# The wide depthwise convolution of a hybrid layer, moved from VectorE to TensorE as products over shifted copies

## The reference, cut to what matters

```python
proj = x @ w_in                      # GLU | q,k,v | output gate | beta | decay | branch gates
u  = glu[:, :512] * sigmoid(glu[:, 512:])
cv = causal_dwconv(conv_hist, u, w_dw) + b_dw      # 512 channels, 31 taps, per group of tokens
A  = silu(layer_norm(cv)) @ w_conv_out             # branch A
q, k, v = split(silu(causal_dwconv(qkv_hist, qkv, w_short)))       # 4 taps
q, k = l2_norm(q) * 128 ** -0.5, l2_norm(k)
o, s_new = gated_delta_rule(q, k, v, beta, logdecay, s0)           # 4 heads of 128 x 128
B  = (rms_norm(o) * silu(og)) @ w_dn_out           # branch B
h  = layer_norm(alpha * x + (sigmoid(ga) * A + sigmoid(gb) * B) @ w_o)
# then cross-attention over 256 memory tokens, and a squared-ReLU MLP of width 4096
```

## Time and profile before

| | us |
|---|---|
| median of 3 runs (1341.56 to 1355.39) | 1348.65 |
| profiled execution, its own time | 1354.72 |
| its span, first to last instruction | 1352.9 |
| PE busy in the span | 1216.4 (90%) |
| DVE busy | 728.7 (54%) |
| ACT busy | 410.0 (30%) |
| POOL busy | 418.0 (31%) |
| mean granted TensorE clock | 0.937 of full |

### The profile page before, as it was taken

How to read it: one execution, slowest core, us unless ns; L and a number is a source line. 1 busy time by engine, 2 the same in 40 slices (tenths; PEclk the granted TensorE clock), 3 DMA queues, 4 the chain that set the end, 5 groups by cost and what they waited for, 6 DMA issues and landing times.

```text
span 1352.9 us, 21587 instructions
## 1 busy us (share of the span) xinstructions
PE 1216.4 (90%) x8713; PEld 1155.0 (85%) x8713; DVE 728.7 (54%) x1140; ACT 410.0 (30%) x675; POOL 418.0 (31%) x193
## 2 busy tenths in 40 slices
PE   6986998888889889999979997969999999999993
PEld 6984788888889769999979865958999999999992
DVE  4775565898799864448690141896212211211257
ACT  4335210211212324223463241345213312312312
POOL 3331123011111204334555300445433332433422
PEclk9998688898889979999989998989999999999997
DMA  6111212011110332232347253211222222222201
GB/s 221 64 62 47 99 32 78 32 32 32 31 32 32 64 9 80 91 109 79 109 125 264 93 235 156 78 47 63 78 82 81 88 79 79 78 85 83 83 32 70
DMA packets 37490, 112.14 MB, mean 83 GB/s; under 512 B 12192, under 2 KB 12704, under 8 KB 34976
## 3 DMA queue, kind: packets, MB, share of 16 engines
q1 hardware_dynamic: 31520, 105.77, 23.4%
q10 hardware_dynamic: 5888, 5.18, 2.0%
HBM read 103.40 MB, written 7.53 MB: 82 GB/s over the span
## 4 chain that ended last, share of the span: by engine, by line
PE 63%; DVE 14%; issue 2%; DMA 2%; ACT 2%; SPq 0%; ACTq 0%; DVEq 0%
PE bank L374 51%; PE bank L582 5%; DVE cv L1242 3%; PE bank L385 1%; DVE res L1691 1%; PE bank L760 1%; PE bank L706 1%; DVE res L1689 1%; DMA kv<-v 1%; DVE lns L1678 1%; PE bank L722 1%; DMA kv<-kT 1%; PE bank L742 1%; DVE h_lo L1684 0%; PE bank L468 0%
## 5 line engine op out<-in xcount | busy, mean ns | idle before, releaser
L338 POOL TENSOR_TENSOR w_lo<-w_raw,w_hi 128x1024 fp32r<-128x1024 f32 x152 | 384.7, 2533 | 851.0 <-ACT w_hi L843 851.0
L843 ACT ACTIVATE w_hi<-w_raw 128x1024 fp32r<-128x1024 f32 x152 | 160.5, 1057 | 273.6 <-PE bank L374 232.1
L374 PE MATMUL bank<-x_hi,w_hi 128*128 128x288 f32 x640 | 204.2, 319 | 16.0 <-DVE x_lo L1225 8.4
L374 PE MATMUL bank<-x_lo,w_hi 128*128 128x288 f32 x640 | 196.3, 307 | 0.0
L374 PE MATMUL bank<-x_hi,w_lo 128*128 128x288 f32 x640 | 195.6, 306 | 0.0
L374 PE MATMUL bank<-h_hi,w_hi 128*128 128x288 f32 x608 | 181.0, 298 | 4.9 <-issue 2.7
L374 PE MATMUL bank<-h_lo,w_hi 128*128 128x288 f32 x608 | 180.0, 296 | 0.0
L374 PE MATMUL bank<-h_hi,w_lo 128*128 128x288 f32 x608 | 179.4, 295 | 0.0
L374 PE MATMUL bank<-hid_hi,w_hi 128*128 128x288 f32 x496 | 146.8, 296 | 0.0
L374 PE MATMUL bank<-hid_lo,w_hi 128*128 128x288 f32 x496 | 146.3, 295 | 0.0
L374 PE MATMUL bank<-hid_hi,w_lo 128*128 128x288 f32 x496 | 145.8, 294 | 0.0
(11 more groups left out here) (346 smaller groups left out, 2322.9 us busy)
## 6 DMA issues: line engine op xcount, KB each, us to landing
w_raw<-w SPq DMA_DIRECT2D x152, 512.0 KB, 3.4
kv<-kT SPq DMA_DIRECT2D x8, 1024.0 KB, 6.9
kv<-v SPq DMA_DIRECT2D x8, 1024.0 KB, 9.3
xraw<-xT SPq DMA_DIRECT2D x4, 576.0 KB, 6.0
yT<-res SPq DMA_DIRECT2D x8, 288.0 KB, 2.2
sst<-sdelta SPq DMA_DIRECT2D x4, 512.0 KB, 6.6
sdelta_out<-sst ACTq DMA_DIRECT2D x4, 512.0 KB, 2.6
memraw<-memT SPq DMA_DIRECT2D x1, 1024.0 KB, 4.8
```

The lines of the kernel that those rows point to most:

```text
L338: nc.gpsimd.tensor_tensor(wlo[:, s], raw[:, s % RAW], whi[:, s].bitcast(f32), sub)\
L374: ins = nc.tensor.matmul(bank[:, 0:b - a], lhsT=w[:, slot, kb], rhs=m[:, kb, a:b], start=(opens and i == 0 and j == 0), stop=(closes and i ...
L843: A_(whi[:, c % RING], raw[:, c % RAW], ACT.Copy).then_inc(hi_ready, 1)
```

## The change

Four items of the wide convolution ("conv") are put among the chunks of the filler, and DVE's taps are gone. For each block j of 128 channels SP makes 16 DMAs from `u` into `u4`: partition 32t + c of `u4[:, g]` is channel 32g + c, shifted by t tokens. DVE builds stationary tiles `wst` (128 rows: 4 taps of 32 channels; 32 columns: the channels), so that one product adds four taps of 32 channels, and its output goes to a quarter of the partitions, hence to a quarter of the array's columns. Eight such groups of taps, four quarters, and three pieces of tokens (288, 224 and the samples' 64) make 96 products in f32 for a block, in four slices. ACT empties the banks into `cv`, with the bias. `u4` is one buffer: the copies of block j wait for the products of block j - 1 (`conv_done`).

The items come in a new order (`ITEMS`), the calls of `between` are placed anew on all three engines, and SP's list of loads is written out around the copies. `own8`, `kown` and the product with them go; in their place the states are the stationary operand, and the samples' values are corrected before they are flipped.

```diff
+ITEMS = [("gate", 0), ("glu", 0), ("gate", 1), ("glu", 1), ("conv", 0), ("gate", 2), ("glu", 2), ("conv", 1), ("gate", 3),
+         ("glu", 3), ("conv", 2), ("og", 0), ("og", 1), ("conv", 3), ("og", 2), ("og", 3)] + [("ga", i) for i in range(8)]
...
+    wst = at("wst", R1 + 13.25, [P, 2, 4, TAPS4, 32])
+    u4 = at("u4", R1 + 21.25, [P, 4, UP + DEC_BATCH * US])
...
+        for t in range(4):                                  # SP, after the loads of chist
+            for g in range(4):
+                a = PAR["w_dw"] + t
+                n = CT * CONV_K - t
+                sp.dma_start(w4[32 * t:32 * t + 32, g, 0:n], A["par"][32 * g:32 * g + 32, a:a + n])\
+                    .then_inc(S("cst_loaded"), 16)
+        def shifted(j):
+            sp.wait_ge(*emptied(("glu", j)))
+            if j:
+                sp.wait_ge(S("conv_done"), j)
+            for t in range(4):
+                for g in range(4):
+                    sp.dma_start(u4[32 * t:32 * t + 32, g, 0:U4], u[32 * g:32 * g + 32, j, t:t + U4])\
+                        .then_inc(S("u4_loaded"), 16)
...
-        weights(4, C_GLU + 8)
+        weights(4, C_GLU + 4)
+        load_w(C_GLU + 4)
+        load_w(C_GLU + 5)
         sp.wait_ge(S("qraw_free"), 1)
         for h in range(HEADS):
             sp.dma_start(sst[h][:], A["sdelta"][:, h]).then_inc(S("sst_loaded"), 16)
-        weights(C_GLU + 8, C_WO + 4)
+        load_w(C_GLU + 6)
+        for j in range(CT):
+            shifted(j)
+            load_w(C_GLU + 7 + 2 * j)
+            load_w(C_GLU + 8 + 2 * j)
+        load_w(C_GLU + 15)
+        weights(C_GLU + 16, C_WO + 4)
...
+        def conv_taps(j, bank, at, taps, src):              # PE
+            for q in taps:
+                for g in range(4):
+                    ins = nc.tensor.matmul(at(bank[32 * g:32 * g + 32]), lhsT=wst[:, j % 2, g, q], rhs=src(u4[:, g], 4 * q),
+                                           start=(q == 0), stop=(q == TAPS4 - 1))
+            return ins
+        def conv_slice(j, n, out):
+            first, second = range(0, TAPS4 // 2), range(TAPS4 // 2, TAPS4)
+            taps = second if n % 2 else first
+            if n < 2:
+                return conv_taps(j, out[0], lambda b: b[:, 0:HALF], taps, lambda s, k: s[:, k:k + HALF])
+            ins = conv_taps(j, out[1], lambda b: b[:, 0:SEQ - HALF], taps, lambda s, k: s[:, k + HALF:k + SEQ])
+            if n == 3:
+                ins = conv_taps(j, out[1], lambda b: tiled(b[:, SEQ - HALF:HALF], DEC_SEQ), range(TAPS4), ...)
...
+                if kind == "conv":                          # PE's filler
+                    pe.wait_ge(S("u4_loaded"), 16 * 16 * (i + 1))
+                    pe.wait_ge(S("wst_ready"), i + 1)
...
             sum_rows((ps[4], ps[5]), 0, i, l2s[:, i % 2], i == 0, i == 2 * HEADS - 1).then_inc(S("l2_sum"), 1)
+            if i % 2:
+                between()
...
             spread((ps[6], ps[7]) if i % 2 == 0 else (ps[4], ps[5]), i, l2r[:, 0]).then_inc(S("l2_bc"), 1)
+            if i % 2:
+                between()
...
-                ins = T.matmul(ps[6][SL, h * DK:(h + 1) * DK], lhsT=kown[:, h, b], rhs=sst[h][:, b], ...)
+                ins = T.matmul(ps[6][:, h * SAMPLE + 8 * b:h * SAMPLE + 8 * b + 8], lhsT=sst[h][:, b],
+                               rhs=qkv[:, HEADS + h, SEQ + 8 * b:SEQ + 8 * b + 8], start=True, stop=True)
...
-        between()                                           # PE, after s_yz and after s_o
+        between(2)
...
+                if kind == "conv":                          # ACT's filler
+                    act.wait_ge(S("conv_done"), i + 1)
+                    for h, half in enumerate(HALVES):
+                        ins = A_(cv[:, i, half], out_pair(o)[h][:, 0:HALF], ACT.Identity, bias=pc("b_dw", i))
+                    ins.then_inc(taken[o % 2], 1)
...
-        between(SLICES + 2)                                 # ACT and DVE, after the L2 roots
+        between(2 * SLICES)
...
+        def stationary(j):                                  # DVE
+            if j == 0:
+                own.step(V.tensor_reduce(fold[:], ident.rearrange("p (t c) -> p c t", c=32), X, add))
+                own(V.memset(w4[96:128].rearrange("p g (j k) -> p g j k", k=CONV_K)[:, :, :, CONV_K - 3], 0.0))
+            if j >= 2:
+                dve.wait_ge(S("conv_done"), j - 1)
+            ...
+            V.tensor_tensor(wst[:, j % 2], mine.unsqueeze(3).broadcast_to(shape),
+                            fold[:].unsqueeze(1).unsqueeze(1).broadcast_to(shape), mul).then_inc(S("wst_ready"), 1)
...
+                    if i == 0:                              # DVE's filler, after u of block i
+                        stationary(0)
+                        stationary(1)
+                    elif i > 1:
+                        stationary(i)
...
-        def between(n=1, taps=2):
+        def between(n=1):
             for _ in range(n):
                 next(fill, None)
-            wide_taps(taps, written[0])
...
-            between()                                       # DVE, the prompt's part, after the decays
+            between(3)
...
-        between(FILL * SLICES)
-        wide_taps(len(todo), CT)
+        between(len(ITEMS) * SLICES)
```

More of the change, by code:

```diff
@@ L49, with item_place, item_chunk @@
 CHUNKS = 152
-O_QKV, O_GLU, O_OG, O_GA, O_GB, O_WO, O_MEM, O_XQ, O_XO, O_FF = 0, 12, 20, 24, 32, 40, 48, 64, 72, 80
-FILL = C_MIX - C_GLU
+O_QKV, O_GLU, O_GB, O_WO, O_MEM, O_XQ, O_XO, O_FF = 0, 12, 36, 44, 52, 68, 76, 84
 SLICES = 4
+TAPS4 = (CONV_K + 3) // 4
+ITEMS = [("gate", 0), ("glu", 0), ("gate", 1), ("glu", 1), ("conv", 0), ("gate", 2), ("glu", 2), ("conv", 1), ("gate", 3),
+         ("glu", 3), ("conv", 2), ("og", 0), ("og", 1), ("conv", 3), ("og", 2), ("og", 3)] + [("ga", i) for i in range(8)]
+def item_place(item):
+    return O_GLU + ITEMS.index(item)
+def item_chunk(item):
+    before = ITEMS[:ITEMS.index(item)]
+    return C_GLU + len([i for i in before if i[0] != "conv"])
 GROUPS, GT = DEC_BATCH // 4, 4 * DEC_SEQ
@@ L211, in build, with emptied @@
     N_STORES = 1 + 1 + 2 * CT + 2 + KB
-    CONSTS = 13
+    CONSTS = 14
+    CST_LOADS = 2 + CT + 16
+    U4 = UP + DEC_BATCH * US - 2
+    def emptied(item):
+        o = item_place(item)
+        return taken[o % 2], o // 2 + 1
     def at_head(pr, hh):
@@ L442, in filler @@
+        def filler():
+            for item in ITEMS:
+                kind, i = item
+                o = item_place(item)
+                if kind == "conv":
+                    pe.wait_ge(S("u4_loaded"), 16 * 16 * (i + 1))
+                    pe.wait_ge(S("wst_ready"), i + 1)
+                else:
+                    c = item_chunk(item)
+                    pe.wait_ge(lo_ready, c + 1)
                 pe.wait_ge(taken[o % 2], o // 2)
                 for n in range(SLICES):
-                    ins = gemm(c % RING, out_pair(o), x, every[2 * n:2 * n + 2], opens=(n == 0), closes=(n == SLICES - 1))
@@ L556, in _ @@
         ins.then_inc(S("s_o"), 1)
-        between()
+        between(2)
         for h in range(HEADS):
@@ L944, in _ @@
         ch.step(A_(sw[SL, S_D], sw[SL, S_D], ACT.Exp))
-        act.wait_ge(S("s_products"), 4)
-        A_(sz[SL], ps[7][SL, :], ACT.Copy).then_inc(S("s_z"), 1)
-        between(4)
+        between(6)
         between()
@@ L953, in _ @@
         between()
-        between(2)
+        act.wait_ge(S("s_products"), 4)
+        A_(sz[SL], ps[7][SL, :], ACT.Copy).then_inc(S("s_z"), 1)
+        between(4)
         act.wait_ge(S("s_o"), 1)
         A_(qkv[:, 2 * HEADS:, ST], tiled(ps[5][:, 0:4 * SAMPLE], SAMPLE), ACT.Copy).then_inc(S("s_otaken"), 1)
-        between()
+        between(2)
         for h in range(HEADS):
@@ L988, in _ @@
                 between()
-        between(FILL * SLICES)
-        act.wait_ge(S("cv_taps"), 2 * CT * CONV_K)
+        between(len(ITEMS) * SLICES)
+        act.wait_ge(*emptied(("conv", CT - 1)))
+        act.wait_ge(*emptied(("conv", CT - 2)))
         act.wait_ge(S("o_taken"), at_tile(1, TILES - 1, 1))
@@ L1267, in _ @@
         dve.wait_ge(S("consts"), CONSTS)
[L1268 to L1277, removed]
[L1278 to L1281 removed]
+        dve.wait_ge(S("cst_loaded"), 16 * CST_LOADS)
+        own = Chain(dve, "dve_own")
+        def stationary(j):
[4 more added lines that the diff above has]
+                dve.wait_ge(S("conv_done"), j - 1)
+            shape = [P, 4, TAPS4, 32]
+            mine = w4[:, :, j * CONV_K:(j + 1) * CONV_K].rearrange("p g (o k) -> p g o k", o=1)[:, :, 0, 0:CONV_K:4]
+            V.tensor_tensor(wst[:, j % 2], mine.unsqueeze(3).broadcast_to(shape),
+                            fold[:].unsqueeze(1).unsqueeze(1).broadcast_to(shape), mul).then_inc(S("wst_ready"), 1)
         def filler():
[L1284 to L1285 removed]
+            for item in ITEMS:
+                kind, i = item
+                o = item_place(item)
                 for _ in range(SLICES - 1):
                     yield
[L1288 to L1292 removed]
```

(16 more changed lines are left out.)

125 lines of the change are left out of this document (56 added, 69 removed).

## The result

The changed kernel is slower: 1364.8 us against 1349.7 for the kernel before on the same chip, a ratio of 1.012 (95% interval 1.006 to 1.018). A second series gave 1355.1 against 1349.8, 1.007 (1.003 to 1.010). The forecast was 7 us faster, a ratio of 0.995.

What follows compares the result with a forecast made beforehand. PE's weight products make half the last-ending chain; PE is busy 309 of 350 us and waits for DVE behind taps. Terms +3.4 +10 +1 -20.7 -2.2 +1.5 give -7.0 us, from 1348.65 to 1341.6; range 1318 to 1364.

Steps and rivals of the forecast that it cites:

- the first pair: First pair of tiles, 238.1 to 363.2 us: start, levels and tiles shorten without taps, -20.7 us (-14 to -24).
- the second: Second pair, 363.2 to 466.7 us: start and levels shorten, tiles get three more slices, together -2.2 us.
- the start: Kernel start: 16 small tap loads ahead of chunk 4's weights delay ACT's split, +3.4 us (nothing to +18.7).
- The price of a conv item: PE's products for one convolution block: 9.2 us an item, four are 37; by the ends 34 to 44.
- that rival: Copies into `u4` come late and PE waits for them: 1371 us, chance 0.12.
- the quarters run side by side: Conv products in four array quarters overlap; rival that they don't: +28 us an item, 1450 us, chance 0.02.
- three signs of being wrong: PE waiting for DMAs, a conv item over 11 us, or the first pair not shortening by 14.
- the end: After the second pair: two slices left over and two chunks for ACT to empty before its squares, +1.5 us.
- the norms and the samples: Norms: slices added and spreading lengthened, +10 us (+6 to +20); samples: conv slices against saved waits, +1, within 6.
- The loop's bounds of 14.1 and 28.2: Norms' spreading with four slices: 14.1 us if the clock holds, 28.2 if not; 18 taken.
- the clock holds: Rival: slices keep PE at 2.4 GHz through norms and samples, -22 us, 1327 us, chance 0.22.
- the base: Sum made from one profiled execution, 1354.72 us, 6.1 above the median shown; forecast taken from 1348.65.

Runs made afterwards that it cites:

- run three: Changed kernel with ACT's eight squares of the norms ahead of the last two chunks' emptying: 1355.2 us, 0.9995 to the kernel before.
- runs two and three: Run two: changed kernel with the sixteen `w4` loads later in SP's queue, 1358.7 us, 1.004 to the kernel before; run three has its own line.
- the second profile: The changed kernel run again, unaltered: spreading loop 15.7 us instead of 26.4, norms and samples together 128.4 us.
- run seven: Kernel before with 120 of 124 taps of the wide convolution left out on DVE: 1314.5 us, 0.974 to the kernel before.
- Run twelve: Changed kernel with five earlier edits, plus GpSimd's next low parts waiting until the samples' states are renewed: 1341.2 us, 0.993 to the kernel before.

## Why the prediction was wrong

**Right, with its mechanism:** the first pair (-20.7; -19.7 and -20.4), where PE's waits behind taps went and the levels became dense; the second (-2.2; -3.4 and -2.1); the start (+3.4; +3.6 and +4.5), by the chain of chunk 4 that was named. Two of these sizes agree in part by luck. The parts of the first pair make up for one another: in the first profile its start fell by 1.9 us (5.5 forecast), its levels by 5.9 (5.4), its tiles by 11.9 (9.8). And the 16 loads took 9.1 us, not 7.0, behind four issues that took 4.2 instead of 5.6.

The price of a conv item was 9.2 us and came out at 2.08 + 2.08 + 1.65 + 2.54 = 8.35: 65 ns for 288 columns (63 predicted), 52 for 224 (50); only the samples' 64 columns, 0.89 us for 64 instructions, 14 ns, lay under the 17 to 57 allowed (the 30 taken was a quarter of 112 ns, the row with 128 columns behind a load; with eight columns it is 122). A change of tiling mode costs nothing that these rows show. The copies of a block took 11 us to issue, 0.69 us each where 0.4 was counted, and landed 2.8 us after their issue, so some 14 us instead of 10, but PE never waited for them: that rival is out, and the quarters run side by side. SP's queue, the copies of block 1:

```profile
190.19 10.96 SPq L323 DMA_DIRECT2D u<-u  x16
```

None of the three signs of being wrong that the prediction named came: no wait for a DMA, an item of 8.35 us, a first pair 20 us shorter. They watched the new products and the first pair, and the time was lost elsewhere. The first series lies 0.8 us above the range, the second inside it.

**The step that failed first is the end.** The prediction had both facts, two slices over and two chunks to empty ahead of the squares, and priced them at +1.5, without saying how. They cost 6.7 to 7.1, and run three took them away by moving eight instructions. What was mis-sized is ACT's delay: ACT can't empty the last chunk before PE's trailing slices (4.81 us) are done, and its last sigmoid waits 2.97 us for them. So the first square starts 6.4 us after PE's last state product (472.95 and 466.58), where it was 0.4 before (467.08 and 466.69). From there to DVE's last addition it is 4.8 us in both kernels. The rest, 1.2 us, is PE's: its twenty products behind the wait of 4.94 us took 6.70 us instead of 5.54.

**Second, the norms and the samples, +11 together.** The means of the four profiles of this order (the changed kernel twice, runs two and three) are +12.1 and +3.9, within the bounds given (+6 to +20; within 6), but both over what was taken. The loop's bounds of 14.1 and 28.2 were sound: it was seen at 15.7 and at 26.4. Taking 18, nearer the lower end, had no row behind it; the only row there was, 0.56 under the same products, pointed the other way. The rival "the clock holds" came true for the norms of the second profile alone, and the samples of that execution still stood at 0.86. In the samples one wrong term can be named: the prediction let most of the 5.30 us of wait ahead of the first pair go with the taps. 3.8 us of it stayed in every profile of the changed kernel, and 4.37 in run seven without the taps. Run twelve shows its cause: POOL's low parts hold DVE up there, a tap before the change and the state's decay after it. The new wait for gate 1's banks, 1.5 forecast, was 2.3 in both profiles.

**Third, the base.** The sum was made against one execution and taken off the median, 6.1 us below it. The two profiles after stand 8.6 and 0.3 us above the profile before, while the medians differ by 15 and 5: most of that gap is the profile of before having run long, by 2 to 5 us against the medians of 1349.7 to 1352.8 that its kernel showed beside these runs. In which stage isn't shown; there is one profile of it.

By the means of all profiles of that order in which a stage was unaltered, the terms give +4.3 + 12.1 + 3.9 - 19.7 - 2.5 + 7.4 + 0.8 = +6.3. With 2 to 5 for the base that is 8 to 11 us, where the two ratios (0.7% and 1.2%) say 9 and 16. What separates the two series isn't settled beyond the scatter of the clock.

Run seven gives the other side of the sum: the taps cost the kernel before 35 us by medians; in the profiles (that of before ran long) 24.4 in the first pair, 7.6 in the second, 6.4 in the samples. The prediction's own terms, before what it charged for new products, come to some 26, 5 and 10 there, so it saw what there was to win, and too much of it in the samples. It erred on what the change pays: products and delays in the places that the taps left.

## What to carry to other kernels

When work moves to the engine that is already nearly full, price what it displaces there, and follow each displaced step both ways, back to all that it has to wait for and on to the last engine that waits for it. Where a stage runs at a mix of the two clock levels, take its mean and its bounds from several executions: two profiles of one kernel differed by 11 us in a loop of some 20. And look at a long row of VectorE for what GpSimd does beside it: on top of the other edits, what brought this kernel under the one before was one wait added on GpSimd.

## What the runs showed of the hardware

- The granted clock fell to 0.50 for 20 us in which PE was busy 20.00 of 20.00 us, under products with eight rows and weight slices between them; the same instructions ran at 1.00 in another execution.
- Taking work off PE need not shorten a stage by as much: with 7/8 of the conv products gone the samples ran at 0.71 in one profile, 0.80 to 0.88 with them in four, and gained 2 us.
- 64 instructions of 128x8 in a row took 8.6 to 11.6 us in nine profiles, and 7.3 at a clock of 1.00 in three with two weight slices among them (groups of 16, 32 and 16).
- Products of 32 stationary columns over 64 columns, in four quarters in turn, each with its own load, follow each other at 14 ns.
- A VectorE instruction that takes 1.21 us with GpSimd idle took 6.38 beside GpSimd instructions that ended 5.30 us after its start.
